# Attention pairs beside dense products: where the second dense piece of a trip stands

## The reference, cut to what matters

```python
# first block, 8 heads each, S = 512
s = einsum(q_chunk, k_band) * scale + bias;  p = softmax(s);  ya = (p @ v) * silu(ga)
s = einsum(qb, k_selected) * scale;          p = softmax(s);  yb = (p @ v) * silu(gb)
gate_a = sigmoid(za + b_merge[0])            # za = xn @ w_in columns: the dense work beside it
# second block, layer 0
m = memory_attention(z[..., -256:], ...)     # 4 heads, keys and values from 256 memory rows
i = h @ hg_w_in columns 1536:2304            # the mixer's values hv: the dense work beside it
```

## Time and profile before

| what | value |
|---|---|
| median of three runs | 1872.19 us |
| time of the profiled execution | 1874.77 us |
| its span, first to last instruction | 1873.0 us |
| TensorE matmul busy | 1747.3 us (93%) |
| VectorE, ACT, POOL busy | 893.0, 760.1, 699.6 us |
| mean granted TensorE clock | 0.963 |
| span of `ab` on TensorE | 204.3 to 329.3 us |
| span of `m0` on TensorE | 617.5 to 671.7 us |

### The profile page before, as it was taken

The page is one execution under the profiler, slowest core; times in us unless marked ns, Lnnn a source line. Parts: engine busy times, 40 slices in busy tenths (PEclk is TensorE's granted clock), DMA queues, the critical chain, the costliest instruction groups (busy, mean ns, idle before and its releaser), DMA issues.

```text
span 1873.0 us, 24838 instructions
## 1 busy us (share of the span) xinstructions
PE 1747.3 (93%) x8605; PEld 1420.2 (76%) x8605; DVE 893.0 (48%) x1675; ACT 760.1 (41%) x1167; POOL 699.6 (37%) x362
## 2 busy tenths in 40 slices
PE   5999899998689989889999999998887999999999
PEld 4778566887668778778888888887755788888887
DVE  3587565457534236554555541143454355555200
ACT  4333455323335424444545443324423354444322
POOL 2344211443333346514444444543300244444444
PEclk9999899999789979899999999999988899999999
DMA  4233211232222211012323233332200123332333
GB/s 178 84 108 101 63 40 35 90 111 92 79 67 90 79 45 35 23 34 91 101 90 100 90 101 106 108 96 68 74 5 1 56 91 94 97 101 90 101 106 118
DMA packets 43278, 151.75 MB, mean 81 GB/s; under 512 B 4929, under 2 KB 5057, under 8 KB 43073
## 3 DMA queue, kind: packets, MB, share of 16 engines
q1 hardware_dynamic: 41184, 145.16, 24.7%
q10 hardware_dynamic: 2016, 5.53, 0.9%
HBM read 148.58 MB, written 2.10 MB: 80 GB/s over the span
## 4 chain that ended last, share of the span: by engine, by line
issue 53%; POOL 23%; PE 21%; DVE 1%; ACT 1%; DMA 1%; POOLq 1%; ACTq 0%; DVEq 0%
POOL WL L541 22%; PE DB L617 4%; PE DB L618 3%; PE DB L619 3%; PE SC L912 2%; PE SC L717 1%; PE DB L742 1%; PE OB L731 1%; PE TB L617 1%; PE DB L731 1%; DMA CONST<-in_consts_dram 1%; PE TB L618 0%; PE TB L619 0%; PE DB L669 0%; PE DB L667 0%
## 5 line engine op out<-in xcount | busy, mean ns | idle before, releaser
L541 POOL TENSOR_TENSOR WL<-RAW,WH 128x1024 fp32r<-128x1024 f32 x268 | 643.5, 2401 | 1161.4 <-ACT WH L1104 1161.4
L1104 ACT ACTIVATE WH<-RAW 128x1024 fp32r<-128x1024 f32 x268 | 283.7, 1059 | 731.5 <-PE DB L619 307.0
L617 PE MATMUL DB<-XH,WH 128*128 128x512 f32 (+1 forms) x616 | 256.2, 416 | 11.7 <-DVE XL L1548 6.5
L972 PE MATMUL DB<-XH,WH 128*128 128x512 f32 x640 | 249.0, 389 | 0.0
L973 PE MATMUL DB<-XL,WH 128*128 128x512 f32 x640 | 249.0, 389 | 0.0
L974 PE MATMUL DB<-XH,WL 128*128 128x512 f32 x640 | 249.0, 389 | 0.0
L618 PE MATMUL DB<-XL,WH 128*128 128x512 f32 (+1 forms) x616 | 243.8, 396 | 0.0
L619 PE MATMUL DB<-XH,WL 128*128 128x512 f32 (+1 forms) x616 | 243.1, 395 | 0.0
L617 PEld LDWEIGHTS DB<-XH,WH 128*128 128x128 f32 x616 | 120.6, 196 | 51.0 <-issue 19.1
L619 PEld LDWEIGHTS DB<-XH,WL 128*128 128x128 f32 x616 | 120.6, 196 | 24.9
L972 PEld LDWEIGHTS DB<-XH,WH 128*128 128x128 f32 x640 | 120.1, 188 | 25.1
(11 more groups left out here) (398 smaller groups left out, 2916.9 us busy)
## 6 DMA issues: line engine op xcount, KB each, us to landing
RAW<-in_stream_dram SPq DMA_DIRECT2D x268, 512.0 KB, 3.5
TP<-in_toep_dram ACTq DMA_DIRECT2D x4, 512.0 KB, 3.7
out_dram<-X SPq DMA_DIRECT2D x8, 256.0 KB, 4.4
X<-in_xt_dram SPq DMA_DIRECT2D x4, 256.0 KB, 5.2
X<-in_xt_dram ACTq DMA_DIRECT2D x4, 256.0 KB, 5.6
MRAW<-in_memt_dram ACTq DMA_DIRECT2D x1, 1024.0 KB, 6.2
CONST<-in_consts_dram ACTq DMA_DIRECT2D x1, 448.0 KB, 9.9
MSKI<-in_masks_dram ACTq DMA_DIRECT2D x1, 288.0 KB, 3.5
```

The source lines that it names most:

```text
L541: nc.gpsimd.tensor_tensor(WL[:, s, :], RAW[:, j, :], WH[:, s, :].bitcast(F32), ALU.subtract).then_inc(lo_done, 1)
L617: mm(o, WH[:, s, c], hi(k), start=(k == 0), stop=False)
L972: mm(o, WH[:, s, c], xh(k), start=(k == 0), stop=False)
L1104: A(WH[:, n % SPLIT, :], RAW[:, n % RING, :], ACT.Copy).then_inc(hi_done, 1)
```

## The change: where the second piece is issued

The loop that took `pieces` pieces (two in both places) in front of the value products becomes one piece in front of them, and one piece between them and the transposes. The parameter `pieces` goes. The number of pieces per trip and in all, their order and all other instructions stay.

```diff
-            def attention(seg, banks_read, beside=None, pieces=1):
+            def attention(seg, banks_read, beside=None):
...
-                    for _ in range(pieces if beside is not None and k >= 2 else 0):
+                    if beside is not None and k >= 2:
                         next(beside, None)
                     if k >= 3:
                         pair = seg[k - 3]
...
                         last.then_inc(pv_done, 1)
+                    if beside is not None and k >= 2:
+                        next(beside, None)
                     if 2 <= k < n + 2:
                         pair = seg[k - 2]
...
-            attention(segments["ab"], [emptied("gb3")], itertools.chain(*(feature_tiles(f"za{k}", xh, xl) for k in range(KD))), 2)
+            attention(segments["ab"], [emptied("gb3")], itertools.chain(*(feature_tiles(f"za{k}", xh, xl) for k in range(KD))))
...
-            attention(segments["m0"], [], itertools.chain(*(token_tiles(f"hv{k}", xh, xl, 384) for k in range(2))), 2)
+            attention(segments["m0"], [], itertools.chain(*(token_tiles(f"hv{k}", xh, xl, 384) for k in range(2))))
```

## The result

The changed kernel took 1881.04 us (median of 5 runs, 1879.12 to 1881.32), the kernel before beside it 1872.70 us (5 runs, 1869.97 to 1877.27): ratio 1.0039, 95% interval 1.0023 to 1.0055. By the ratio that is slower by 7 us, where 2.2 us was forecast, and 1881.04 us lies outside the range of 1870.4 to 1877.1 us.

The account below looks back on a forecast made before the run. TensorE's own instruction sequence was taken as the bound, with no wait to fill. Seams +1.9 us and waits +0.3 us made +2.2 us, 1874.4 us against the median of 1872.19, range 1870.4 to 1877.1 us.

Parts of the forecast that it names:

- how the numbers follow: Whole kernel: chance 0.79 within 0.2%, 0.16 slower, 0.05 faster; time 1874.4 us.
- rival 3: Values to dense: dense product pays nothing in mid trip, transposes' gain stays; -1.8 us, 1870.4 us; chance 0.13.
- rival 1: Seams: dense product costs the whole 0.105 us, transposes give nothing back; +4.3 us, 1876.5 us; chance 0.12.
- rival 4: Full trips of `ab`: ACT's copies slip, value products reached too soon; +4.9 us, 1877.1 us; chance 0.04.
- about 0.2%: Whole kernel: a measurement tells about 0.2%, 3.7 us, from no change.
- The sum: Both stretches: seams +1.9 us and waits +0.3 us give +2.2 us, 0.12%.
- Seams: 38 trips of `ab` and `m0`: dense product +0.105 us, transposes -0.055 us, together +0.05 us a trip.
- Waits in trips 32 and 33: `ab` without scores as cover: value products wait on ACT's copy 0.06 and 0.27 us.
- The bank wait in trip 7: `m0`: value products of pair 4 wait 0 to 0.1 us for the first group's bank; taken as 0.
- The waits of 1.1 and 2.4 us: Last trip of `ab` on ACT's copy, trip 6 of `m0` on the first `hv` evacuation; both to stay.
- Rival 2: Around the value products: the piece hides both seams; -5.2 us, 1867.0 us; chance 0.05.

Follow-up runs that it names:

- the one-place kernel: One piece on each side of the value products in `ab` alone, `m0` keeping two in front, against the kernel before: ratio 1.0021.
- the kernel with both pieces behind: Both pieces put between the value products and the transposes, in `ab` and `m0`, against the kernel before: ratio 1.0060.
- the cut in the value products: First piece in front of the value products, second in their middle where there are two or more key tiles, against the kernel before: ratio 1.0060.
- the one with the delay: The kernel before plus eight overwritten dense products between `ab` and the next job, no seam changed: ratio 1.0011.

## Why the prediction was wrong

**The step that failed** is that of how the numbers follow: "The range goes down to rival 3 at 1870.4 and up past rival 1 to rival 4, 1877.1". The range was built from the bounds of the change's own costs around a median of three runs, and the clock behind the two stretches was put at nothing without a reason; only a fall inside them was named. The runs put in its place that this kernel's time, with no change at all, lies anywhere from 1869.4 to 1877.8 us, by how much of it is granted the lower clock, and the changed kernel's from 1870.0 to 1881.5 us. In the two profiles the stretches give 2.1 us and the low-clock places outside them the other 4.4 us. For the same reason "about 0.2%" was too fine for five runs against five.

**The sum was right inside the two stretches,** where TensorE ran at full clock in both profiles. Seams: +0.05 us a trip forecast, +0.045 us measured. Both halves are in the trace of after: +0.105 us on the dense product, 0.05 us back on the transposes. Waits in trips 32 and 33: 0.06 and 0.27 us forecast; 0.06 and 0.27 us measured. `ab` in all: +1.9 us forecast, +1.74 us measured (1.79 us in the one-place kernel). `m0`: 0.35 us forecast, 0.37 us measured. The bank wait in trip 7: 0 to 0.1 us forecast and taken as 0, 0.06 us measured. The forecast let the value products start 0.05 us after VectorE's last row, a distance read behind ACT; behind VectorE it is 0.15 us, which with the earlier trace rows gives 656.39 against 656.32, a wait of 0.07 us. The 0.37 us of `m0` so hold 0.31 us of seams, and that it meets the 0.35 us is in part luck. The waits of 1.1 and 2.4 us stayed. For the whole kernel three of four measurements give +1.9 to +2.2 us at equal clock (+2.6 to +2.9 us against the 24 runs of the kernel before that ran as kernels of their own, which stand 0.7 us under the others). Since the gap goes from 0.1 to 4 us with the clock, this meeting with the sum's +2.2 us is in part luck too; the trace of the two stretches is the better witness.

**The rivals.** Rival 1 (whole seam, 4.3 us) is refuted by the transposes' 0.05 us in every trip. Rival 2 (both seams hidden) too: 0.33 us stands ahead of the value products as before. Rival 3 (nothing on the dense product) by 317.52 to 317.86. Rival 4 (copies slip): no wait on ACT in full trips; the kernel with both pieces behind shows what it would have looked like. By the rule of the Trainium skill, page "TensorEngine Tiling (Array Packing)", section Key Properties, that changing the mode drains the engine, the change costs nothing, the cut in the value products costs, and pieces ahead of the scores save one change of mode per trip (three instead of four). The trace agrees in the sign of the last two, at 0.35 and 0.20 us, and differs by the 0.045 us that the change does cost. No run tells a drain from weight loads that are not covered as the cause of a seam's price: the prices are shown, their cause is argued.

**What stays open.** The first five runs of the change were all at a clock of 0.961 to 0.963. Of the 36 later ones 13 were. If each run draws by itself, five in a row have a chance of 0.36^5, under 1%. They were on another occasion; no run here tells whether that matters. That at equal clock they stand at +3.8 +- 0.5 us, 1.6 us above the later sets, is at least in part the one slope: the three of them at 0.961 average 1881.22 us, the four later ones at 0.961 1881.33 us. What is shown is that 7 us is not what the change costs on average: it did not come back as the mean of three sets of twelve. Why the change has a group of runs at 1879 to 1881.5 us that the kernel before lacks stays open.

## What to carry to other kernels

Where TensorE never waits, look for the price of a schedule where narrow products (64 rows or 64 columns) border on full ones. Here an order with as many such borders cost 0.045 us more; putting narrow runs side by side saved 0.2 us a trip, and cutting one with dense work cost 0.35 us. Count the seams in the order as written, and read the price of each at its own first distance, its own last one and its own neighbour. Before a difference under 0.5% is believed, set each run's time against its granted clock and run the old kernel as often as the new one. Then give the raw ratio too, since the clock itself can go with the kernel.

## What the runs showed of the hardware that was not expected

- The time of one and the same program goes with its mean granted clock: 1.13 us for 0.001 in the kernel before, 1.65 us in the changed one, 1.27 us with one slope for all kernels. A thousandth of 1873 us of clock is 3.7 us at the lower level, so a microsecond at the lower level costs 0.30, 0.44 and 0.34 us of time. That is less than the 0.5 us that a TensorE busy throughout would lose; that part of it falls where TensorE is not the bound would explain this, but is not shown.
- Kernels that differ can share one course of the clock: the kernel with one piece on each side in `ab` and the one with the delay had 129 us at the lower level each in their profiled executions, in nearly the same places, and spans of 1871.4 and 1871.1 us. And a kernel can have a course of its own: the one with both pieces ahead of the scores in `ab` and `m0` had a clock of 0.960 to 0.962 in all twelve runs.
- A run of value products has an end of about 0.15 us: 4 take 0.37 us to the next start, 8 0.59, 12 0.81 and 16 1.03 us. That is 0.055 us for each of them and 0.15 us once.
